# Stick-breaking attention: the weights-times-values products of a group of four rows issued in one step of four instead of in two halves

## The reference

```
def sb_attend(q, q_pos, k, v, k_pos):
    z = jnp.einsum('bqhd,bkhd->bhqk', q, k, preferred_element_type=jnp.float32) * (SB_HEAD_DIM ** -0.5)
    mask = (k_pos[None, :] < q_pos[:, None])[None, None]
    log_keep = jnp.where(mask, jax.nn.log_sigmoid(-z), 0.0)
    suffix = lax.cumsum(log_keep, axis=3, reverse=True) - log_keep
    a = jnp.where(mask, jnp.exp(jax.nn.log_sigmoid(z) + suffix), 0.0)
    return jnp.einsum('bhqk,bkhd->bqhd', a.astype(v.dtype), v)
```

## Time and profile before

| | us |
|---|---|
| median of 3 runs | 2969.64 (2969.59 to 2970.26) |
| the profiled execution: its own time | 2971.95 |
| the profiled execution: its span | 2970.1 |
| the attention stage of layer 1, within the span | 1783 to 2047 |
| one body of its loop, steps 4 to 4 of the next | 64.23 |

### The profile page before, as it was taken

One profiled execution on the slowest core, in us unless ns is written; L12 is line 12 of the kernel. 1 busy time (PEld: TensorE's weight loads), 2 busy tenths in 40 slices (PEclk: granted clock), 3 DMA queues, 4 the chain that ended last, 5 costly groups with the idle time before them and its releaser, 6 DMA issues. The chain is left out here.

```text
span 2970.1 us, 41820 instructions
## 1 busy us (share of the span) xinstructions
PE 2848.6 (96%) x16003; PEld 2513.9 (85%) x16003; DVE 1160.6 (39%) x1780; ACT 945.8 (32%) x1924; POOL 616.9 (21%) x478
## 2 busy tenths in 40 slices
PE   7979997799999999999899999998999999999998
PEld 6868896689998999899798877775899899989997
DVE  5656662343332333233411007886443233323333
ACT  4334443322211221122312219997131122112212
POOL 3100000112211221122112116664031122112211
PEclk9989998899999999999899999999999999999999
DMA  4211103501110111011134537754011111111111
GB/s 139 83 56 45 42 29 96 184 8 56 58 43 28 42 56 42 28 42 43 68 124 144 157 98 187 179 140 170 1 60 34 40 45 52 32 41 44 54 31 78
DMA packets 191099, 215.49 MB, mean 73 GB/s; under 512 B 17280, under 2 KB 151936, under 8 KB 190976
## 3 DMA queue, kind: packets, MB, share of 16 engines
q1 hardware_dynamic: 190976, 213.82, 23.8%
HBM read 166.17 MB, written 47.61 MB: 72 GB/s over the span
## 5 line engine op out<-in xcount | busy, mean ns | idle before, releaser
L1485 DVE TENSOR_TENSOR x<-m_ps,x 128x512 f32<-128x512 f32 x324 | 223.9, 691 | 607.8 <-PE m_ps L76 607.8
L1521 DVE TENSOR_TENSOR m_sq<-m_relu 128x384 f32<-128x384 f32 x192 | 170.7, 889 | 504.9 <-ACT m_relu L1417 504.9
L74 PE MATMUL m_ps<-h_h,m_up0h 128*128 128x384 f32 x768 | 257.0, 335 | 0.0
L76 PE MATMUL m_ps<-h_h,m_up0l 128*128 128x384 f32 x768 | 256.7, 334 | 0.0
L75 PE MATMUL m_ps<-h_l,m_up0h 128*128 128x384 f32 x768 | 256.6, 334 | 0.0
L74 PE MATMUL m_ps<-h_h,m_up1h 128*128 128x384 f32 x768 | 256.5, 334 | 0.0
L75 PE MATMUL m_ps<-h_l,m_up1h 128*128 128x384 f32 x768 | 256.5, 334 | 0.0
L76 PE MATMUL m_ps<-h_h,m_up1l 128*128 128x384 f32 x768 | 256.5, 334 | 0.0
L1417 ACT ACTIVATE m_relu<-m_ps 128x384 f32<-128x384 f32 x192 | 94.5, 492 | 507.2 <-PE m_ps L76 507.2
L1412 ACT CAST m_dn0h<-m_dn_raw 128x1024 fp32r<-128x1024 f32 x16 | 16.8, 1051 | 546.9 <-PE m_ps L76 546.8
L1465 POOL TENSOR_TENSOR m_dn0l<-m_dn_raw,m_dn0h 128x1024 fp32r<-128x1024 f32 x16 | 38.2, 2390 | 528.0 <-ACT m_dn0h L1412 528.0
(11 more groups left out here) (503 smaller groups left out, 7193.9 us busy)
## 6 DMA issues: line engine op xcount, KB each, us to landing
m_up_raw<-in_mlp_w_up SPq DMA_DIRECT2D x64, 512.0 KB, 4.7
m_dn_raw<-in_mlp_w_down SPq DMA_DIRECT2D x64, 512.0 KB, 3.4
h_raw<-scratch_oT SPq DMA_DIRECT2D x4, 1536.0 KB, 14.6
scratch_qr<-a_qrst SPq DMA_DIRECT2D x9, 512.0 KB, 3.4
a_x<-in_x_prompt SPq DMA_DIRECT2D x8, 512.0 KB, 5.0
b_qr<-scratch_qr SPq DMA_DIRECT2D x4, 1024.0 KB, 6.9
scratch_oT<-b_o SPq DMA_DIRECT2D x32, 128.0 KB, 1.7
new_p_sb_k<-d_rows SPq DMA_DIRECT2D x16, 256.0 KB, 2.1
```

Source lines behind the costliest of these rows:

```text
L74: pe.matmul(out, w[0], m[0], start=start, stop=False)
L76: return pe.matmul(out, w[1], m[0], start=False, stop=stop)
L1485: dve.tensor_tensor(x[:, t, cols], bank[:, 4 + n % 3, :], x[:, t, cols], ALU.add).then_inc(added.sem, 1)
L1521: dve.tensor_tensor(sq[n % 2][:], relu[n % 2][:], relu[n % 2][:], ALU.mult).then_inc(sq_done.sem, 1)
```

## The change

The function `values` issues all products of a group at once. It is called in step 4g + 6, where the second half stood; in step 4g + 4 nothing is called. The waits of both halves stand ahead of the one block. No other engine's instructions change.

```diff
-    VALUES = ((0, 4, 8), (0, 3, 7), (0, 2, 6), (0, 2, 5))
...
-            def values(i, g, half):
+            def values(i, g):
 
                 pair, short = g // (S.GROUPS // 2), g % 4
-                blocks = S.VALUES[short]
-                t_out[half].wait(pe, TURNS[half] * i + copies(S.before(4 * g + 4), half))
-                if half == 0:
-                    if g % (S.GROUPS // 2) == 0:
-                        v_in[pair].wait(pe, 16 * (i + 1))
-                    o_done.wait(pe, S.GROUPS * i + g)
-                for k in range(blocks[half], blocks[half + 1]):
+                for u in range(2):
+                    t_out[u].wait(pe, TURNS[u] * i + copies(S.before(4 * g + 4), u))
+                if g % (S.GROUPS // 2) == 0:
+                    v_in[pair].wait(pe, 16 * (i + 1))
+                o_done.wait(pe, S.GROUPS * i + g)
+                for k in range(NPT - short):
                     cols = slice(0 if k <= short else P, GQ)
                     for a in range(2):
                         rows = slice(a * SB_DIM, (a + 1) * SB_DIM)
                         done = pe.matmul(bank[rows, 7, cols], v[pair][:, k, rows], turned_block(g, a, k, k <= short),
                                          start=k == 0, stop=k == NPT - 1 - short)
-                if half == 1:
-                    done.then_inc(pv_done.sem, 1)
+                done.then_inc(pv_done.sem, 1)
...
-                    if j == 0 and values_of is not None and values_of % 2 == 0:
-                        values(i, values_of // 4, values_of % 4 // 2)
+                    if j == 0 and values_of is not None and values_of % 4 == 2:
+                        values(i, values_of // 4)
```

## The result

| | before | after |
|---|---|---|
| median of 14 runs each, us | 2969.86 (2967.05 to 2973.52) | 2976.54 (2973.71 to 2978.62) |
| profiled execution, own time | 2971.95 | 2973.71 |
| its span | 2970.1 | 2971.9 |
| first to last output copy (L2272, now L2271) | 1804.0 to 2046.2, 242.2 | 1800.8 to 2048.0, 247.2 |
| one body of the loop | 64.23 | 65.52 |

What follows compares the result with a forecast made beforehand. PE, busy 96% of the span, was taken as the bound, its lead limited by banks. +0.74 us a body, +3.0 over four bodies, plus 0.4 at the stage's end gave +3.4: median 2973.0 us, range 2961 to 2980.

Steps and rivals of the forecast that it cites:

- It can run ahead only as far as the three task banks and four score banks allow: Steps 4g + 4 to 4g + 6: banks limit PE's use of given-back time, up to 1.24 us in group 4.
- The 0.50 us that the first half of group 3 waited: Group 3: this wait for ACT's copy moves to the sample task, which needs the same bank; group cost +0.01 us.
- The costs of groups 0 to 6: Moved stream less PE's earlier arrival at the block: +0.30, +0.45, -0.34, +0.01, +0.16, +0.46, -0.34 us.
- the old distance from these transposes to the block: Groups 0 and 1: time from stopped transposes to the second half, carried over unchanged as 1.30 and 1.36 us.
- Group 7, the same pattern, +0.04: Last group of a body: same stops as group 3, costing +0.04 us.
- The stage's end: Last groups, no scores left to fill PE: loss between nothing and 0.84 us, taken as 0.4.
- The sum: All eight groups: +0.74 us a body, +3.0 us for four bodies, +3.4 us in total.
- Rival 1: Passages between weight widths saved, bank waits not binding: -2.7 us a body, 2959 to 2962 us; chance 0.2.
- Rival 2: A block of 1.9 us starves ACT: all groups cost 0.46 or 0.23 us, 2981 us; chance 0.28.
- Rival 3: PE and ACT coupled, order irrelevant: 2969.6 us, give or take 2; chance 0.52 together with the forecast.
- Expected signs: Profile after: unbroken block, L2516's ACT waits gone, copy and scan waits in groups 0, 1, 4, 5, body 65.0 us.
- A reading of before: Old trace: 0.17 us idle at each passage between 128-, 64- and 32-wide weights, none between 128-wide kinds.

Runs made afterwards that it cites:

- e1: Changed kernel with the three task banks going on in turn over the bodies, instead of the last task taking bank 1: 2972.8 us, ratio 1.0008.
- e5: e1 with sample tasks `scores` and `turn` written to the free half of bank 7, not the three task banks: 2972.18 us, ratio 1.0005.
- e8: Kernel before with only groups 2 and 6 in one block, the others in halves: 2969.81 us, ratio 0.9999.
- e9: Kernel before with all groups but 2 and 6 in one block: 2978.08 us, ratio 1.0026.
- e10: Kernel before with groups 1 and 5 alone in one block: 2973.56 us, ratio 1.0012.
- e4: Kernel before with one key block in the first half of every group, the rest in the second: 2971.06 us, ratio 1.0002.
- e3: Changed kernel with the block at the end of odd step 4g + 5 instead of in step 4g + 6: 2986.64 us, ratio 1.0053.
- e7: Kernel before with the sample task of each even step ahead of the half instead of behind it: 2976.96 us, ratio 1.0023.

## Why the prediction was right, and where it was off

- *"It can run ahead only as far as the three task banks and four score banks allow"* is shown. Taking away one bank stop in the seam (e1) gives back what it cost, taking away others (e5) moves the stop to the score bank and lowers the costs of groups 1 and 5 by 0.2 us each, and which groups are joined decides the sign (e8 to e10) although every block is equally long. The 0.50 us that the first half of group 3 waited moved to the sample task, as the prediction said (L2451 at 1884.13).
- *The costs of groups 0 to 6* came out within 0.18 us each, 0.43 measured for 0.70 forecast in sum. Groups 0, 1 and 5 were put 0.08 to 0.18 us high, and not because copies came earlier: the stopped transposes start 4.97, 5.07 and 4.85 us behind the sample task before them, where the forecast's old copy times give 4.98, 5.07 and 4.86. Too long was the old distance from these transposes to the block: 1.13, 1.25 and 1.25 us, where 1.30, 1.36 and 1.35 were carried over. Behind a stop the two transposes of group 1 load in 0.20 us, in full flow they took 0.32.
- *"Group 7, the same pattern, +0.04"* failed: +0.86 us. Group 7 ends at the seam, where its sample task needs not the bank of ACT's copy, three tasks back, but that of DVE's copy, two tasks back. The trace before had it: `keys` at 1919.20 stood behind the half with DVE's copy named as releaser. I had read it as the passage, as it was no longer than one. This one term is 0.82 us at each of three seams, 2.5 us of the 5.0 by which the stage grew; by the medians of e1 it may be up to 3.6 of the 6.7.
- *The stage's end.* 0.4 us was a choice between nothing and 0.84. In the last body group 6 costs +0.39 us where it gains 0.31 in the others, 0.7 us in all.
- *The sum.* +0.74 us a body was +1.29. The median's +3.4 us was +6.7, and the stretch between the output copies shows 5.0 of it: the forecast's 3.4, less 1.1 for groups 0 to 6, plus 2.5 for three seams and 0.3 for the end, is 5.1. So the range held with some luck: two terms too small and three too large met in it. The median lies 3.5 us above the forecast and 4.5 us below the second rival's 2981, and alone could not have decided between them; the costs by group do.
- *Rival 1*, the passages saved: 19 idle stretches of 0.17 us at the block for 38 are seen, but a body got longer and not shorter. What groups 2 and 6 gain fits the passages saved there.
- *Rival 2*, ACT starved in every group: ACT does run dry behind every block, as said above. But the costs are not the 0.46 or 0.23 us in all groups that this rival has, and e4, e8 and e10 speak against it. A schedule in which ACT starves far more is e3, 4.1 us a body slower than before.
- *Rival 3*, nothing moves: the bodies of the kernel before agree within 0.04 us and the changed ones are 1.29 us longer, so the order does matter.
- *Expected signs.* The block came in one piece of 1.9 us. ACT's waits for scores "above 14 us" were 11.2; those for sample pieces rose instead. The waits of L2516 for ACT were to be gone, and 1.5 of 5.9 us are left. The waits of transposes for copies came in groups 0, 1, 4 and 5 as named.
- *A reading of before.* The idle 0.17 us were said to stand "not between two 128-wide kinds of work". A like stretch does: the mask's weights (L2435), 128 wide behind 128-wide scores, load late too, by 0.16 to 0.28 us in the rows of one body. The change leaves these rows as they were, so no term of the sum hangs on it.

```profile
PEld e_ps L2435 <- issue: 14.5, 64, 0.5
```

## What to carry to other kernels

Joining two bursts on the busiest engine can save its passages, but here the time that this gave back could only be used as far as buffers let the engine run ahead. Look, for each place where the burst leaves, at which buffer the very next instruction needs, and at what time that was freed before: a half that stood there may have covered the wait. A schedule of repeating groups need not take one form in all of them, as joining paid in two groups of eight (not in the last body) and cost in the others; and where a ring of buffers doesn't divide the loop, look at the seam by itself. And check a sum term by term: e4 hit its sum with the cost in another group than expected.

## What the runs showed of the hardware

The passage between 128-, 64- and 32-wide weights on TensorE was 0.16 to 0.17 us of idle weight loading in most rows of every kernel here. It was 0.20 us from the sample `values`' 32-wide weights back to 128-wide ones, 0.23 from those of the sample `scores`, and 0.38 behind a half that ends with 256-column products. The Trainium skill (TensorEngine Tiling (Array Packing), section Key Properties) says that a change of the tiling mode, and not of the tile alone, drains TensorE. The trace agrees in that such a stretch stands at each of these changes; the mask's rows above show that idle weight loading stands elsewhere too. Unexpected was how exactly the loop repeats, the three bodies of a run within 0.13 us of each other, while the runs of one kernel spread over up to 7 us (2975.04 to 2982.08 in e7) and the stage's first scores started anywhere from 1780.0 to 1784.1 us in the profiled executions: a change of a few microseconds is better read in the loop's period than in the span.
